# A three-layer diffusion block on one core: the norm weights after layer 1 are folded into layer 2, and the engines enter a layer at the last down product

## The reference

```python
h_lat = modulate(x_lat, m_lat[0], m_lat[1])          # x * (1 + scale) + shift
h_ctx = modulate(x_ctx, m_ctx[0], m_ctx[1])
...                                                   # y = attention(h) @ w_out
x_lat = layer_norm(DN_ALPHA * x_lat + m_lat[2] * y_lat, ln_g[l, 0], ln_b[l, 0])
f_lat = conv_ffn(modulate(x_lat, m_lat[3], m_lat[4]), ffn_w_up[l], ffn_conv_w[l], ffn_conv_b[l], ffn_w_down[l])
x_lat = layer_norm(DN_ALPHA * x_lat + m_lat[5] * f_lat, ln_g[l, 1], ln_b[l, 1])
if ctx_out:                                           # the same two steps for x_ctx, layer 1 alone
    ...
```

## Time and profile before

| quantity | value |
|---|---|
| median of 3 runs | 2598.48 us (2597.49 to 2601.83) |
| the profiled execution | 2600.93 us |
| its span in the trace | 2599.1 us |
| PE busy | 2405.3 us, 93% of the span |
| DVE / ACT / POOL busy | 1625.2 / 974.8 / 365.9 us |
| mean granted TensorE clock | 0.965 of full |

### The profile page before, as it was taken

One profiled execution on the slowest core, in us unless ns is written; L12 is line 12 of the kernel. 1 busy time (PEld: TensorE's weight loads), 2 busy tenths in 40 slices (PEclk: granted clock), 3 DMA queues, 4 the chain that ended last, 5 costly groups with the idle time before them and its releaser, 6 DMA issues.

```text
span 2599.1 us, 33349 instructions
## 1 busy us (share of the span) xinstructions
PE 2405.3 (93%) x13242; PEld 1928.7 (74%) x13242; DVE 1625.2 (63%) x2761; ACT 974.8 (38%) x1768; POOL 365.9 (14%) x355
## 2 busy tenths in 40 slices
PE   7988998999989899998989999999979898999996
PEld 3865567888878777565768888888867676888875
DVE  3448676565765641888767765656464885765455
ACT  4335453322212421666343231322332773423232
POOL 0110103010021100000300123123141000000123
PEclk9999999999999899999989999999989999999998
DMA  6231125554443221100311332333122103332321
GB/s 238 92 102 49 33 66 191 206 179 137 159 150 121 98 68 52 58 30 15 132 55 65 130 114 97 106 121 115 57 89 66 42 2 128 132 113 81 106 90 49
DMA packets 79002, 255.48 MB, mean 98 GB/s; under 512 B 5632, under 2 KB 10368, under 8 KB 70400
## 3 DMA queue, kind: packets, MB, share of 16 engines
q1 hardware_dynamic: 65024, 203.44, 22.6%
q0 software_dynamic: 12528, 45.62, 5.1%
q10 hardware_dynamic: 1296, 4.30, 0.4%
HBM read 243.89 MB, written 9.44 MB: 97 GB/s over the span
## 4 chain that ended last, share of the span: by engine, by line
PE 69%; DVE 14%; ACT 6%; issue 4%; POOL 1%; DMA 0%; DVEq 0%; POOLq 0%; ACTq 0%
PE PS L975 9%; PE PS L977 9%; PE PS L976 9%; PE PS L1011 5%; PE PS L1012 5%; PE PS L1013 5%; PE PS L746 3%; PE PS L743 3%; PE PS L744 3%; PE PS L843 3%; PE PS L856 2%; PE PS L885 2%; PE PS L952 2%; ACT HT L2216 2%; PE PS L950 2%
## 5 line engine op out<-in xcount | busy, mean ns | idle before, releaser
L975 PE MATMUL PS<-HH,WH 128*128 128x512 f32 x1056 | 417.8, 396 | 7.6 <-DVE WL L1836 5.9
L976 PE MATMUL PS<-HL,WH 128*128 128x512 f32 x1056 | 414.6, 393 | 0.0
L977 PE MATMUL PS<-HH,WL 128*128 128x512 f32 x1056 | 414.3, 392 | 0.0
L2079 ACT ACTIVATE WH<-STG 128x1024 fp32r<-128x1024 f32 (+1 forms) x204 | 198.9, 1023 | 304.9 <-PE PS L1013 240.2
L1836 DVE TENSOR_TENSOR WL<-STG,WH 128x1024 fp32r<-128x1024 f32 (+1 forms) x204 | 239.3, 1214 | 47.5 <-ACT WH L2079 47.3
L1011 PE MATMUL PS<-WH,AH 128*128 128x512 f32 x616 | 246.0, 399 | 13.4 <-DVE WL L1836 5.0
L1012 PE MATMUL PS<-WL,AH 128*128 128x512 f32 x616 | 244.2, 396 | 0.0
L1013 PE MATMUL PS<-WH,AL 128*128 128x512 f32 x616 | 243.8, 396 | 0.0
L975 PEld LDWEIGHTS PS<-HH,WH 128*128 128x128 f32 x1056 | 200.8, 190 | 50.8 <-issue 7.5
L976 PEld LDWEIGHTS PS<-HL,WH 128*128 128x128 f32 x1056 | 200.8, 190 | 42.2 <-issue 1.0
L977 PEld LDWEIGHTS PS<-HH,WL 128*128 128x128 f32 x1056 | 200.5, 190 | 42.3
(11 more groups left out here) (213 smaller groups left out, 4365.6 us busy)
## 6 DMA issues: line engine op xcount, KB each, us to landing
STG<-in_w_up SPq DMA_DIRECT2D x66, 1024.0 KB, 6.9
ADAW<-in_w_ada SPq DMA_DIRECT2D x96, 512.0 KB, 4.0
STG<-in_w_down SPq DMA_DIRECT2D x20, 1024.0 KB, 5.1
ADAW<-in_w_ada POOLq DMA_DIRECT2D x32, 512.0 KB, 4.2
STG<-in_w_ffn_out SPq DMA_DIRECT2D x10, 1024.0 KB, 7.1
STG<-in_ev_w_in SPq DMA_DIRECT2D x8, 1024.0 KB, 5.1
spill<-X POOLq DMA_DIRECT2D x14, 512.0 KB, 4.9
STG<-in_w_in SPq DMA_DIRECT2D x6, 1024.0 KB, 5.5
```

The costliest lines, as they stand in the source:

```text
L975: e.matmul(PS[:, b, 0:T], h_, HH[gi][:, c, :], start=first, stop=False)
L976: e.matmul(PS[:, b, 0:T], h_, HL[gi][:, c, :], start=False, stop=False)
L977: return e.matmul(PS[:, b, 0:T], l_, HH[gi][:, c, :], start=False, stop=last)
```

## The change

Four things are changed together.

1. The multiplication by `g` and the addition of `b` after the last norm of layer 1 are left out of that stage. `x_ready(2, tt)` becomes the end of ACT's normalisation. The weights go into layer 2's modulation instead: when its scale vector arrives, three short DVE instructions of 8 columns make `shift + scale * b` and `scale * g`, for both sets of tokens; the columns of `ln_g[0, 1]` and `ln_b[0, 1]` are fed in transposed with `cols`.
2. The tiles that were stored without the weights get them in `w_out` of layer 2, when they are back: DVE multiplies and adds over four tiles of 1024 columns. `g` and `b` are fetched for this by POOL after layer 2's projections, where before they were fetched in the middle of layer 1's feed-forward stage.
3. DVE and ACT no longer wait for all four ends of the feed-forward stage before layers 1 and 2, but for PE's last down product (DVE for POOL's end too).
4. `turn_x` for the first set of tokens is put ahead of `split(L, 0, 1)` in layers 1 and 2, as it already was in layer 0; `turn_place` of layer 1 moves.

```diff
+    def block_multiplied(self, L):
+        return self.pe_down((L, len(CHUNKS[L]) - 1, 1, GROUPS[L][-1][1][-1]))
...
@@ weights_free
-        return [self.pe_up((L - 1, last, len(GROUPS[L - 1]) - 1, 1))] if h == 0 else self.ends(("ff", L - 1))
+        return [self.pe_up((L - 1, last, len(GROUPS[L - 1]) - 1, 1))] if h == 0 else [self.block_multiplied(L - 1)]
@@ x_ready
-        return self.ln_ready("f", 1, tt)
+        return self.ac_ln(("f", 1, tt))
@@ vector_program, ada
-                    if layer == 0 or j != 4:
+                    if (layer, j) not in ((1, 4), (2, 1), (2, 4)):
...
                     e.tensor_tensor(k.mod(0, 1, 2), sc, b, ALU.mult).then_inc(*k.dv_fold.up((layer, v, j, 1)))
                     w.wait_ge(*k.dv_fold((layer, v, j, 1)))
                     e.tensor_tensor(sh, sh, k.mod(0, 1, 2), ALU.add).then_inc(*k.dv_fold.up((layer, v, j, 2)))
                     e.tensor_tensor(sc, sc, g, ALU.mult).then_inc(*k.dv_mod.up((layer, v, j)))
@@ vector_program and scalar_program, project
-        if L == 0:
-            have.add(1)
-            turn_x(0, 1, CTX)
+        vec = int(UNITS[L][0][3] < 2)
+        have.add(vec)
+        turn_x(L, vec, CTX if vec else LAT)
         split(L, 0, 1)
@@ vector_program, layer_norm
-        if stage == "a":
+        if stage == "a" or L == 1:
             return
@@ vector_program, w_out
+        if L == 2:
+            gain = k.ln_gain("f", 1)
+            for i, tt in enumerate(WOUT_TT[L]):
+                old = k.reg(L, 2048 + i * 1024, 3072 + i * 1024)
+                w.wait_ge(*k.old_in[tt](("wo", L)))
+                w.wait_ge(*k.lg_in[0](("f", 1)))
+                e.tensor_tensor(old, old, gain[:, 0:1024], ALU.mult).then_inc(*k.dv_old.up(("mul", i)))
+                w.wait_ge(*k.dv_old(("mul", i)))
+                w.wait_ge(*k.lg_in[1](("f", 1)))
+                e.tensor_tensor(old, old, gain[:, 1024:2048], ALU.add).then_inc(*k.dv_old.up(i))
...
@@ vector_program, before layers 1 and 2
-        for s in k.ends(("ff", L - 1)):
-            w.wait_ge(*s)
+        w.wait_ge(*k.block_multiplied(L - 1))
+        w.wait_ge(*k.pl_end(("ff", L - 1)))
         project(L)
@@ gpsimd_program, layer_norm
-        if tt == last_tile(L):
+        if L == 1 or tt == last_tile(L):
             return
@@ gpsimd_program, after the wait for layer 2's last projection
+        if L == 2:
+            gains("f", 1)
```

More of the change, by code:

```diff
@@ L163, in __init__ @@
                 F["YS"] = self.LOW
[L164 to L167, removed]
             self.ff.append(F)
@@ L208, in __init__ @@
         self.dv_fold = sig("dv_fold")
+        self.dv_old = sig("dv_old")
         self.dv_g = sig("dv_g")
@@ L411, in ln_gain @@
     def ln_gain(self, stage, L):
-        return self.ff[L]["LG"] if stage == "f" else self.LOW
+        return self.LOW if stage == "a" else self.reg(2, 8192, 10240) if L == 1 else self.ff[L]["LG"]
     def window(self, nk):
@@ L1439, in ada @@
                                                op0=ALU.add, op1=ALU.add)
-                    if layer == 0 or j != 4:
+                    if (layer, j) not in ((1, 4), (2, 1), (2, 4)):
                         m.then_inc(*k.dv_mod.up((layer, v, j)))
                         continue
[L1443 to L1448, removed]
+                    m.then_inc(*k.dv_fold.up((layer, v, j, 0)))
+                    i_sh, i_ln = (0, 1) if j == 1 else (2, 2 * layer - 2)
+                    sh, sc = k.mod(layer, v, i_sh), k.mod(layer, v, i_sh + 1)
+                    g, b = (k.cols("lg", 16 * i_ln + 8 * x, 8) for x in range(2))
+                    w.wait_ge(*k.dv_fold((layer, v, j, 0)))
+                    e.tensor_tensor(k.mod(0, 1, 2), sc, b, ALU.mult).then_inc(*k.dv_fold.up((layer, v, j, 1)))
+                    w.wait_ge(*k.dv_fold((layer, v, j, 1)))
+                    e.tensor_tensor(sh, sh, k.mod(0, 1, 2), ALU.add).then_inc(*k.dv_fold.up((layer, v, j, 2)))
                     e.tensor_tensor(sc, sc, g, ALU.mult).then_inc(*k.dv_mod.up((layer, v, j)))
@@ L2690, in ffn @@
                     e.tensor_tensor(y[1], y[1], y[0], ALU.mult).then_inc(*k.pl_gate.up((L, pi, gi)))
-                if L == 1 and pi == ups[-1]:
-                    w.wait_ge(*k.pe_up((1, pi, 1, 1)))
-                    gains("f", 1)
             else:
@@ L2858 @@
          colv(a["ffn_conv_b_2"].reshape(-1)), colv(a["b_ada"][0]), colv(a["ada_b_2"].reshape(-1))]
-        + [colv(a[n].reshape(4, D)[i]) for i in (0, 2) for n in ("ln_g_2", "ln_b_2")], axis=1)
+        + [colv(a[n].reshape(4, D)[i]) for i in range(3) for n in ("ln_g_2", "ln_b_2")], axis=1)
     rows = np.concatenate([a["diff_lambda"].reshape(-1), a["ev_q_gain_2"][0], a["ev_k_gain_2"][0], a["od_sink_2"][0]])
```

6 lines of the change are left out of this document (4 added, 2 removed).

## The result

| | before | after |
|---|---|---|
| median | 2598.64 us (2597.49 to 2601.83, 4 runs) | 2580.10 us (2577.95 to 2584.91, 4 runs) |
| ratio | | 0.9929, 95% interval 0.9912 to 0.9946 |
| profiled execution | 2600.93 us | 2580.57 us |
| span | 2599.1 us | 2578.7 us |
| PE busy | 2405.3 us | 2394.8 us |

The kernel is 18.5 us faster (14 to 23 by the interval of the ratio). So the sign was right, and some 9 us have to be found that the sum did not hold. I go through the places of the sum first.

What follows compares the result with a forecast made beforehand. PE, busy 93% of the span, was taken as the bound, so only its waits could move the time. -9.7 + 1.5 - 1.6 = -9.8 us from 2598.48 gave 2588.7 us (ends 2586.7 and 2592.5; range with rivals 2584.5 to 2595.5).

Steps and rivals of the forecast that it cites:

- The rest: Folding instructions, fetch of g and b, POOL's stores, added input columns: 0 us in all, at most 1.2 + 1.
- The clock term: Passage from layer 1 to 2: the lower clock may last past the new stall, costing 0 to 2.7 us; +1.5 taken.
- chunk 4: Passage from layer 1 to 2: products of chunks 4 to 7 start at 1935.3 instead of 1944.98, -9.7 us.
- The first product of layer 2: Passage from layer 1 to 2: first projection product at 1927.3 instead of 1938.17, about 9.6 us after the last down product.
- the stall for the low half of `PW`: Passage from layer 1 to 2: PE waits 1.2 us for DVE's second half of the weights, before chunk 4.
- The passage from layer 0: Passage to layer 1: DVE starts its chunks 2.0 us earlier, PE's chunks 4 to 7 gain -2.1 us; -1.6 taken.
- the 0.5 that was taken off for the clock: Passage from layer 0 to 1: allowance for a possible 0.9 us clock loss, turning -2.1 us into -1.6.
- The eight instructions: Output product of layer 2: DVE's added work of 9.8 us fits an idle stretch, 0 us, with 0.8 us of cover.
- Rival one: Both passages: PE stays longer at the lower clock, costing 5.4 us more, so -4.4 us, 2594.1; chance 0.13.
- Rival three: Start of layer 2: stored tiles or a weight load hold it, head start 5 us or less, about 2594; chance 0.06.
- Rival two: Output product of layer 2: DVE's new block ends too late, at 2.33 us each +2.2 us, 2600.7; chance 0.07.
- Rival four: Both passages: PE at 2.4 GHz at once, first 24 products gain up to 2.7 each, -14 us, 2584.5; chance 0.08.

Runs made afterwards that it cites:

- experiment 1: The kernel before with 16 unused columns of zeros added, moving every tile behind `COLS` by 64 bytes: 2592.38 us, ratio 0.9972 to the kernel before.
- experiment 2: The changed kernel with `SM` 16 columns shorter, so the tiles behind lie at the old addresses: 2587.90 us, ratio 0.9955 to the kernel before.
- experiment 3: The kernel before with a 64-byte pad ahead of the first tile, so all tiles move together: 2600.10 us, ratio 1.0002.
- experiment 4: All computation left out; TensorE alone multiplies with tiles at different remainders by 128 bytes: 226.7 ns a product at equal remainders, 228.9 to 234.3 otherwise.
- experiment 5: The changed kernel with `SM` 8 columns (32 bytes) shorter, putting `PW`, `HTH` and what lies behind at remainder 96: 2592.13 us, ratio 0.9964 to the kernel before.
- experiment 7: The kernel before with 16 unused columns and only parts 3 and 4 of the change, nothing folded: 2591.88 us, ratio 0.9967 to the kernel before.
- experiment 11: The changed kernel run once more, unedited: 2580.10 us, ratio 0.9917 to the kernel before.
- experiment 6: The changed kernel with parts 3 and 4 undone, the weights still folded: 2580.38 us, ratio 0.9929 to the kernel before.
- experiment 9: The changed kernel with the latent tiles' chunks ahead of the context tiles' last norms before layer 2: 2576.68 us, ratio 0.9908 to the kernel before.
- experiment 10: experiment 9 plus the like reordering before layer 1 and the weights' low half made in two pieces: 2576.24 us, ratio 0.9904 to the kernel before.
- experiment 8: The changed kernel with DVE's new block in layer 2's output product doubled by eight more instructions: 2588.82 us, ratio 0.9961 to the kernel before.

## Why the prediction was wrong, point by point

**The step that failed** is a sentence of "The rest": "The columns added to the input are 8 KB: 0." It costed the columns as a transfer. What they do is move the addresses of every tile allocated behind them by 64 bytes, which brings the operands of some 1,400 products to the same remainder by 128. That is worth 5.6 us in the trace and 7 us (4 to 10) by time, and experiments 1 to 5 show it from both sides. With the columns' own term at 0 and the addresses held (experiment 2), the change is 11.7 us (8.6 to 15.1), and the forecast of 9.8 for its four parts, with its range of 6.0 to 11.8, is not contradicted.

**The clock term was mis-sized.** +1.5 was taken between 0 and 2.7; 0.2 was paid. The clock was back at 1927, before chunk 4. That the loss is real where the clock comes back later is shown by experiment 7, with 1.8 us. What decides between the two was not settled.

**The sum after the fact.** 9.6 + 1.9 + 5.6 - 0.2 = 16.9 us, against 18.5 by the medians. The last product of the profiled execution starts 20.4 us earlier (2555.26 for 2575.61), in the second trace of the changed kernel (experiment 11) 18.6. The rest, 3.5 and 1.7 us, is the balance of stretches at the lower clock that stand in one trace and not in the other, gains and losses. One gain is the 1.0 us (2.3 in the second trace) behind chunk 4 in the passage to layer 1. Another, before:

```profile
2499.00:2506.00 7.00, 7.00 (x20) 5.55 (x20) 4.29 (x7) 1.80 (x2) 4.87 (x4) 0.61 0.42 152
```

and at the same place after:

```profile
2480.00:2487.00 7.00, 6.00 (x26) 4.98 (x27) 6.34 (x9) 3.27 (x5) 4.17 (x3) 1.00 0.41 152
```

No work is moved there, and the kernel of experiment 3, the kernel before in all but a pad and with its time, also has its last product 4.8 us earlier than the profiled execution of before. So I count these as the spread between executions; that a part of them belongs to the change is not excluded.

One loss is no such spread, since it repeats. At the start of layer 2's attention, the clock of the kernel before is back early:

```profile
2024.00:2026.00 2.00, 1.85 (x17) 1.52 (x16) 1.66 (x7) 1.58 (x5) 0.00 (x0) 1.00 0.00 0
```

and at the same work after it is not:

```profile
2007.00:2009.00 2.00, 2.00 (x11) 1.59 (x12) 1.19 (x3) 0.95 (x3) 0.00 (x0) 0.50 0.00 0
```

From the last product of layer 2's projections to the first of its output product the kernel before takes 137.5 us and the changed one 139.9 and 140.1. The kernels of experiments 1, 2, 5, 6, 7, 9 and 10 take 139.9 to 140.9, the one with nothing but the pad among them; those of experiments 3 and 8 take 137.5 and 137.8. The sum of the forecast had no term for these 2.4 us, and their cause is open.

**What held.** The first product of layer 2 was forecast 9.6 us after the last down product and came after 9.7, counted from that product's end as the forecast counts (10.1 from its start); the stall for the low half of `PW` was forecast at 1.2 us and took 0.90; chunk 4 gained 9.6 for 9.7. DVE keeps up with PE, and the 2.33 us addition is 0.69. The passage from layer 0 gave 1.9 at chunk 4 for 2.1, and the 0.5 that was taken off for the clock was not paid. The eight instructions took 1.23 us each and PE does not wait for them, with 1.3 us of cover for 0.8. Rival one did not come about: in the passage to layer 2 the clock was at 1.00 from 1927, and behind chunk 4 of the passage to layer 1 time was gained, not lost. Rival three is out: nothing else held the start. Rival two's mechanism is real, as experiment 8 shows, but its condition (each instruction at 2.33 us) did not come about. Rival four (more than forecast, 2584.5) had the right side, but not by its way: the first 24 products after the hole still ran at a clock of 0.55.

**Which part does what** was not asked by the forecast, and experiments 6 and 7 tell it: the fold gives nearly all of the passage from layer 1, the waits and the order give the 1.7 to 1.9 us of the passage from layer 0. In the passage from layer 1 they are worth up to 0.9 us beside the fold, and by themselves they lose 1.0.

## What to carry to other kernels

An edit that changes the size of any buffer changes the addresses of all behind it; compare the distance between products in stages that the edit does not touch, before the gain is put down to the edit, and pad one way and the other to price it. On in-order engines, put what the bottleneck engine needs next ahead of what it needs later (experiment 9), and expect nothing from an order that leaves the sum ahead of the second need as it was (experiment 10). Work hidden beside another engine is priced by doubling it: the wait that appears, taken from the time by which the work's end moved, gives the cover.

## What the runs showed of the hardware

With all other engines idle, fp32r products of 512 columns follow each other after 226.7 ns when both stationary tiles and the moving one start at the same remainder by 128 bytes, and after 228.9 to 234.3 ns when they do not. In the whole kernel the same distances appear: 227, 231.1 (64/0/64) and 233.3 ns (96/0/96), and the traces put 5.6 and 8.5 us on it, the times 7 and 12, of some 2590. Which period the remainder really has (128 bytes or a multiple), and why addresses matter to TensorE at all, stays open.
